# Attention's gate and queries by seven products of blocks, in a tuned one-core transformer layer

## What is computed

```python
h = rmsnorm(x, norm1_g) * (1.0 + scale1) + shift1
proj = h @ w_in
q_r, k_r, v_r, g_r, q_d, k_d, v_d, gates = split_projection(proj)
gate_r, gate_d = jnp.split(jax.nn.sigmoid(gates + b_gate), 2, axis=-1)
...                                        # rotary positions on q and k of the latent tokens
branch_r = (jax.nn.silu(g_r) * y_r) @ w_ret_out      # y_r: retention, normalised by head
branch_d = o_d @ w_diff_out                          # o_d: differential attention of q_d, k_d, v_d
mix = (gate_r * branch_r + gate_d * branch_d) @ w_o
x = x + gate1 * mix
ffn = (silu(h2 @ w_ffn_gate) * (h2 @ w_ffn_up)) @ w_ffn_down
x = x + gate2 * ffn
```

## Time and profile before

| | |
|---|---|
| median of 3 runs | 1299.69 us (1299.42 to 1299.79) |
| the profiled execution, its own time | 1299.46 us |
| its span | 1297.8 us |
| PE busy | 1259.1 us, 97% |
| DVE busy | 798.2 us, 62% |
| ACT busy | 486.7 us, 38% |
| POOL busy | 300.7 us, 23% |
| PE clock granted | full speed in all 40 slices |
| chain that ended last | 90% on PE |

### The profile page before, as it was taken

The page is one execution under the profiler, slowest core; times in us unless marked ns, Lnnn a source line. Parts: engine busy times, 40 slices in busy tenths (PEclk is TensorE's granted clock), DMA queues, the critical chain, the costliest instruction groups (busy, mean ns, idle before and its releaser), DMA issues.

```text
span 1297.8 us, 19779 instructions
## 1 busy us (share of the span) xinstructions
PE 1259.1 (97%) x7734; PEld 1152.0 (89%) x7734; DVE 798.2 (62%) x1297; ACT 486.7 (38%) x813; POOL 300.7 (23%) x264
## 2 busy tenths in 40 slices
PE   4999999999999999999999999989999999999997
PEld 2698888899999999988788899889998999889986
DVE  4654121477657743374798844478973789557966
ACT  5452233344321122223777622245441344313434
POOL 1002000311000111110799400004510445005500
PEclk9999999999999999999999999999999999999999
DMA  9634222154434434451200234311333133222222
GB/s 309 210 98 138 65 65 82 41 157 136 129 132 130 146 98 130 114 178 50 82 2 1 82 98 146 93 38 33 98 98 97 33 97 99 97 65 66 90 89 81
DMA packets 87394, 129.59 MB, mean 100 GB/s; under 512 B 3529, under 2 KB 64450, under 8 KB 87186
## 3 DMA queue, kind: packets, MB, share of 16 engines
q1 hardware_dynamic: 77024, 95.69, 23.1%
q0 software_dynamic: 8960, 31.68, 8.1%
q10 hardware_dynamic: 1330, 1.10, 0.3%
HBM read 117.43 MB, written 4.73 MB: 94 GB/s over the span
## 4 chain that ended last, share of the span: by engine, by line
PE 90%; DVE 4%; ACT 3%; POOL 1%; issue 1%; DMA 1%; ACTq 0%; DVEq 0%
PE psum L431 31%; PE psum L468 28%; PE psum L687 18%; PE psum L1240 2%; PE psum L1224 1%; PE psum L417 1%; PE psum L1199 1%; PE psum L617 1%; PE psum L1049 1%; POOL probs L989 1%; DVE w_lo L400 1%; DMA rows<-in_diff_subln_g 1%; PE psum L1157 1%; PE psum L1197 1%; POOL probs L995 1%
## 5 line engine op out<-in xcount | busy, mean ns | idle before, releaser
L400 DVE TENSOR_TENSOR w_lo<-w_raw,w_hi 128x2048 fp32r<-128x2048 f32 x57 | 130.6, 2291 | 191.6 <-ACT w_hi L395 189.2
L395 ACT ACTIVATE w_hi<-w_raw 128x2048 fp32r<-128x2048 f32 x57 | 108.8, 1909 | 173.9 <-PE psum L468 107.8
L431 PE MATMUL psum<-h_hi,w_lo 128*128 128x320 f32 x672 | 154.7, 311 | 0.0
L431 PE MATMUL psum<-h_lo,w_hi 128*128 128x320 f32 x672 | 153.1, 309 | 0.0
L431 PE MATMUL psum<-h_hi,w_hi 128*128 128x320 f32 x672 | 153.1, 309 | 0.0
L468 PE MATMUL psum<-w_hi,hid 128*128 128x512 f32 x440 | 135.6, 389 | 0.0
L431 PEld LDWEIGHTS psum<-h_hi,w_hi 128*128 128x128 f32 x672 | 112.4, 188 | 0.0
L431 PEld LDWEIGHTS psum<-h_hi,w_lo 128*128 128x128 f32 x672 | 111.8, 188 | 0.5 <-issue 0.4
L431 PEld LDWEIGHTS psum<-h_lo,w_hi 128*128 128x128 f32 x672 | 112.2, 188 | 0.0
L687 PE MATMUL psum<-h_hi,seven_lo 128*128 128x320 f32 x320 | 98.9, 309 | 1.1 <-DVE silu_g L2296 1.1
L687 PE MATMUL psum<-h_lo,seven_hi 128*128 128x320 f32 x320 | 98.9, 309 | 0.0
(11 more groups left out here) (311 smaller groups left out, 2754.7 us busy)
## 6 DMA issues: line engine op xcount, KB each, us to landing
w_raw<-in_w_in SPq DMA_DIRECT2D x32, 1024.0 KB, 5.6
ada_b<-in_w_ada POOLq DMA_DIRECT2D x32, 512.0 KB, 4.4
w_raw<-in_w_ffn_gate SPq DMA_DIRECT2D x11, 1024.0 KB, 5.3
w_raw<-in_w_ffn_up SPq DMA_DIRECT2D x11, 1024.0 KB, 5.3
ada_a<-in_w_ada SPq DMA_DIRECT2D x8, 1024.0 KB, 13.6
w_raw<-in_w_ffn_down SPq DMA_DIRECT2D x8, 1024.0 KB, 5.1
w_raw<-in_w_ret_out SPq DMA_DIRECT2D x4, 1024.0 KB, 5.2
swapped<-qk_d POOLq DMA_DIRECT2D x32, 128.0 KB, 2.5
```

The source lines that it names most:

```text
L395: act.activation(w_hi[s][:, :, :], w_raw[s][:, :, :], ACT.Copy).then_inc(w_hi_done, 1)
L400: dve.tensor_tensor(w_lo[s][:, :, :], w_raw[s][:, :, :], w_hi[s][:, :, :].bitcast(F32), ALU.subtract).then_inc(w_lo_done, 1)
L431: last = pe.matmul(bank(4 * par + 2 * j + h, HALF), w[:, k, cs], x[:, k, h * HALF:(h + 1) * HALF], start=(k == 0 and n == 0), stop=(k == K ...
```

## The change

`gate_d` and `q_d` are made of seven products, as the up phases are. `ret_out` is moved ahead of `gate_d`. Retention's normalised output is transposed after the second unit of `gate_r` instead of after the fourth. `k_d` takes a set of modulation's vectors in place of `gate_d`. POOL forms the sums of token blocks of `h` in ten subtractions or additions of 128x1280, two of them between each pair of `load_ada` of `ret_out`, and it also multiplies the queries by the cosine. `gate_d`, `qk_d`, `od_hi`, `od_lo`, `v_d`, the rotary tables and the rows of the gates get new addresses, and the gate rows are loaded in two DMAs.

```diff
-          ("gate_r", 4, "act", "act"), ("gate_d", 4, "act", "act"), ("ret_out", 4, "dve", "dve"),
-          ("q_d", 4, "act", "act"), ("k_d", 4, "act", "act"), ("v_d", 4, "act", "act"),
+          ("gate_r", 4, "act", "act"), ("ret_out", 4, "dve", "dve"), ("gate_d", 4, "dve", "dve"),
+          ("q_d", 4, "dve", "dve"), ("k_d", 4, "act", "act"), ("v_d", 4, "act", "act"),
...
-ADA_FIRST = {"gate_r": 0, "gate_d": 4, "ret_out": 8, "v_d": 12}
+ADA_FIRST = {"gate_r": 0, "ret_out": 4, "k_d": 8, "v_d": 12}
+SEVENS = ("gate_d", "q_d", "up0", "up1", "up2")
+GATED = ("gate_d", "q_d")
...
-            pe_dense(pe, "gate_r", pe_T_unit, h_hi, h_lo, first=1)
             pe.wait_ge(y_gated, RH)
-            pe_T_and_dense(pe, "yg", y_nat, "gate_d", h_hi, h_lo)
+            pe_T_and_dense(pe, "yg", y_nat, "gate_r", h_hi, h_lo, i=1)
             pe_dense(pe, "ret_out", pe_T_unit, yg_hi, yg_lo)
-            pe_dense(pe, "q_d", pe_T_unit, h_hi, h_lo)
+            for unit in gated_units:
+                pe_seven(pe, *unit)
             pe_dense(pe, "k_d", pe_T_unit, h_hi, h_lo)
...
+            def add_token_terms(first, end):
+
+                for n in range(first, end):
+                    out, x, y, op = terms[n]
+                    pool.wait_ge(h_sum_step, n) if n else pool.wait_ge(n2t["yg"]["ps"], KT)
+                    pool.tensor_tensor(out, x, y, op).then_inc(h_sum_step, 1)
...
+            add_token_terms(0, 2)
+            for i in range(2):
+                for par in range(2):
+                    load_ada("ret_out", i, par)
+                    add_token_terms(2 + 4 * i + 2 * par, 4 + 4 * i + 2 * par)
+
+            def turn_queries(i, par):
+
+                swap_halves("q_d", qk_d, P // 4, 4, 0, i, par, swapped_d)
+                x = qk_d[:, 4 * i + 2 * par:4 * i + 2 * par + 2, 0:LAT]
+                pool.tensor_tensor(rope_tmp_d[:, :, :], x, rope_d[:, 0:1, :].to_broadcast([P, 2, LAT]), ALU.mult).then_inc(rope_mul, 1)
+
+            for n, unit in enumerate(gated_units):
+                if n == 1:
+                    pool.wait_ge(ada_step, 16 * 9)
+                    pool.dma_start(rope_d[:, :, :], a["const_rope_diff"].rearrange("a p t -> p a t")).then_inc(ld_rope, 16)
+                weight_sums(*unit)
+                if n >= 6:
+                    turn_queries(*gated_units[n - 2][1:])
+                last_weight_sum(*unit)
+            turn_queries(1, 0)
+            pool.wait_ge(mm_done, ready("q_d", 1, 1, 1))
+            load_ada("k_d", 0, 0)
+            turn_queries(1, 1)
...
+            act_split(act, unit_of("ret_out", 1, 0) + 1, 1)
+            for place in range(1, 4):
+                high_of_h_sum(place)
+            prefill("gate_d", (B11, B21, T1, B22), ready("ret_out", 1, 0, 1))
+            prefill("gate_d", (T2, T4, T3), ready("ret_out", 1, 1, 1))
...
+            def gated_unit(n):
...
+                def after_third():
+                    if following:
+                        weights_low(following, (T1, B22, T2))
+                    if n >= 5:
+                        rotate_q(*gated_units[n - 1][1:])
+                    if not following:
+                        dve_split(dve, unit_of("k_d", 0, 0), 0)
...
+            dve.wait_ge(ld_rope, 32)
+            for n in range(len(gated_units)):
+                gated_unit(n)
+            dve_split(dve, unit_of("k_d", 0, 0) + 1, 1)
+            ada_partial("k_d", 0, 0)
+            rotate_q(1, 1)
```

More of the change, by code:

```diff
@@ L142, in ready, with seven_index, is_first_of_sums @@
     return i * 4 + (2 * FIRST[name] + 2 * par + j + 1 + AHEAD)
-def seven_index(third, i, par):
-    return sum(COUNT[f"up{n}"] for n in range(third)) + 2 * i + par
+def seven_index(name, i, par):
+    return sum(COUNT[other] for other in SEVENS[:SEVENS.index(name)]) + 2 * i + par
+def is_first_of_sums(name, i, par):
+    return (i, par) == (0, 0) and name in ("gate_d", "up0")
 def first_tile(third, i):
@@ L1288, in _ @@
                     pe_norm2_and_dense(pe)
-                for unit in units_of(third):
+                for unit in units_of(f"up{third}"):
                     pe_seven(pe, *unit)
@@ L1563, in _ @@
             set_table(ACT.Sigmoid)
             act.wait_ge(norm["normy"]["scaled"], 1)
-            dense_after_split("gate_r", gate("gate_r", mixT, 0))
-            act_to_T(act, "yg", yg_hi, gn_gain)
-            dense("gate_d", gate("gate_d", gate_d, KT))
-            dense("ret_out", lambda i, par: None)
-            dense("q_d", copy_T("q_d", qk_d, 0, DHD ** -0.5))
+            for h in range(RH):
+                normalize_head(h)
+            gate_of_retention(0, 0)
+            act_split(act, unit_of("gate_r", 0, 1) + 1, 0)
@@ L2024, in gated_ret @@
                     dve.tensor_tensor(x, T_tile(4 * par + 2 * j), x, ALU.mult).then_inc(freed["dve"], 1)
-            dense("ret_out", gated_ret)
-            ada_partial("v_d", 0, 0)
-            dve.wait_ge(ld_rope, 32)
-            dense("q_d", rotate("q_d", qk_d, 4, 0, 4, 128))
-            dense("k_d", rotate("k_d", qk_d, 8, DH, 4, 128 + 256))
+            first = gated_units[0]
+            dve_split(dve, unit_of("ret_out", 0, 0) + 1, 1)
+            ada_partial("ret_out", 0, 0)
+            gated_ret(0, 0)
@@ L2031, in _ @@
+            for i in range(2):
+                for par in range(2):
+                    rotate_k(i, par, during_rotation(i, par))
             dense_wide("v_d", nothing)
@@ L2332, in _ @@
                     pending = (0, 0)
-                units = units_of(third)
+                units = units_of(f"up{third}")
                 for n, unit in enumerate(units):
```

448 lines of the change are left out of this document (293 added, 155 removed).

## The result

The changed kernel takes 1305.84 us (median of 5, 1305.39 to 1306.51), the kernel before 1299.69. The ratio is 1.0047, 95% interval 1.0033 to 1.0061: 0.5% slower, where 1291.7 was forecast and 1287.5 to 1297.5 was the range. The profiled execution took 1305.45 us, its span is 1303.8.

What follows compares the result with a forecast made beforehand. The prediction took PE, busy 97% of the span, as the bound. From 1299.46 us, -14.1 + 1.5 + 0.7 + 0 + 3.3 + 0.8 = -7.8 gave 1291.7 us, range 1287.5 to 1297.5.

Steps and rivals of the forecast that it cites:

- Products: Eight units of `gate_d` and `q_d` at seven products, 12.32 us each instead of 14.09: 14.1 us less.
- Retention's output two units earlier: End of `gate_r`'s second unit: ACT and DVE finish the heads with 11 us of room, so 0.
- Last unit of `ret_out`: POOL's token sums delay DVE's low parts and modulation's sums, so PE waits 1.5 us; bounds 0 and 14.
- rival (c): `ret_out`: token sums take 4.7 us, PE waits in every unit, 13.7 us in all; 1303.9 us, chance 0.07.
- First unit of `gate_d`: The rotary table lands late for DVE's read at PE's sixth product: 0.7 us, bounds 0 and 1.5.
- Units of `gate_d` and `q_d`: POOL and DVE are nearly full beside PE, but parts are made a unit ahead: 0, bounds 0 and 5.
- From `q_d` to `k_d`: Rotation on DVE stands before the split of the key weights, so PE waits 3.3 us; bounds 2.5 and 6.
- First key unit: Modulation's sums end late behind DVE's reads and split and POOL's cosine product: 0.8 us, bounds 0 and 2.6.
- (b): Query units overflow on POOL and DVE, three units 1.7 us late each, 5 us more: 1296.7 us, chance 0.15.
- rival (a): POOL hides: modulation's sums don't wait for it, leaving 2.8 us at the split and 0.3 in `gate_d`; 1288.5, chance 0.18.

Runs made afterwards that it cites:

- sums_first: mended with two low parts of the second `gate_d` unit moved behind the first unit's reads on DVE; 1287.46 us, ratio 0.9903.
- ret_end: Changed kernel with DVE's order at the end of `ret_out` changed: modulation's sums ahead of the first two low parts; 1304.61 us, ratio 1.0038.
- late_load: Changed kernel with the 1 MB load of the second key unit's weights held until the swaps have landed; 1300.72 us, ratio 1.0007.
- rot_last: Changed kernel with DVE's query rotations behind each unit's last two reads and low parts, the last behind the key weights' split; 1294.28 us, ratio 0.9954.
- undo_rot: mended with rot_last undone, so rotations stand ahead of the last reads and the split again; 1305.48 us, ratio 1.0041.
- mended: all_edits with DVE's wait for the rotary table moved from ahead of the first `gate_d` unit to the first rotation; 1289.52 us, ratio 0.9926.
- rot_load: rot_last with the 1 MB load of the third key unit's weights held until modulation's columns have landed; 1294.84 us, ratio 0.9958.
- split_first: Changed kernel with only the split of the first key unit's weights moved ahead of the rotation on DVE; 1305.56 us, ratio 1.0046.
- rot_ret: rot_last with ret_end's order at the end of `ret_out`; 1293.65 us, ratio 0.9955.
- rot_ret_load: rot_last with ret_end's order and rot_load's held load; 1292.37 us, ratio 0.9946.
- copy_early: rot_ret_load with ACT's first copy ahead of the high parts and DVE's first read ahead of two low parts in `gate_d`; 1293.97 us, ratio 0.9956.
- cos11: rot_ret_load with the last query pair's cosine product on DVE, behind modulation's sums, instead of on POOL; 1289.57 us, ratio 0.9920.
- all_edits: rot_ret_load with the edits of copy_early and cos11 as well; 1291.03 us, ratio 0.9932.
- no_hold: all_edits without the held load of the third key unit's weights; 1290.47 us, ratio 0.9929.

## Why the prediction was wrong, step by step

- **Products, -14.1: right.** Units of the changed kernel that wait for nothing start 12.32 us apart (403.46, 415.78, 428.10). Without waits of note (sums_first) the kernel is 12.1 us faster: 14.1 less 0.7 of waits, with 1.3 left that no row names.
- **Retention's output two units earlier, 0: right.** PE shows one wait of 0.2 there.
- **Last unit of `ret_out`, 1.5: 1.9 measured, plus 1.5 of clock.** Of the two token sums in a unit the first took 3.0 to 3.2 us (3.1 assumed), the second, in the second and third unit, 4.9 beside DVE's split. That is rival (c)'s rate for one of two, and modulation's sums waited for POOL besides (rows below). In the third unit the sums ended at 370.83, 0.2 us before PE asked. That no wait came there was luck as much as reckoning. In the last unit the two token sums ran alone (3.11 each), and the wait was the forecast's. The half clock behind it was not in the sum.
- **First unit of `gate_d`, 0.7: 0.3.** The table was issued at 394.45 and took 3.9 us, not 5.2; it came before DVE had done the low parts ahead of the read (398.7). PE came late too, by its half clock. In ret_end, at full clock, PE waited 0.6 for this read, behind the same low parts and not for the table. So the size was about right and the cause was another.
- **Units of `gate_d` and `q_d`, 0: 2.6.** The chain named was the right one (rotation, last two reads, ACT's copy, T2), and its time was wrong: the reads ended 8.3 us into the last unit, not 4. DVE's 12.0 us had a rotation at 2.5, and the first took 4.5; it had low parts at 0.89 in the mean, and the one beside POOL's product took 4.11.
- **From `q_d` to `k_d`, 3.3 with bounds 2.5 and 6: this is the step that failed. 10.1, and 2.4 of clock.** It had the order right, the split behind the rotation. It set the rotation's start at 10.5 us into the unit, and it was 19.8 (478.5 to 498.3). 4.2 of these 9.3 us are the late issue: 10.2 into the unit instead of 6, because the previous rotation, late by POOL's holding and by its own swap, held the reads that free ACT. No run takes these two apart. 5.1 are the landing, 9.6 after the first issue instead of 4.5. That 4.5 came from the earlier trace rows, a swap with no weight load beside it (the load issued at 456.1 had landed when it began). late_load gives 5.3 for the same swap with the load held, so the row was nearly right for its neighbourhood and was carried into another. What the runs show in its place: a rotation whose swap is used 9.6 us after its issue holds the reads and the split behind it, and the order alone is worth 11.6 us (rot_last) to 16.0 (undo_rot against mended). The upper bound of 6 should have been worked out with the 1 MB load that T3's low part releases at just this point.
- **First key unit, 0.8: 0,** since PE came so late itself. In rot_last, where PE is on time, it is 1.5, within the bounds.

The second unit of `ret_out` in the changed kernel, POOL and DVE:

```profile
344.79 4.91 POOL L1053 TENSOR_TENSOR h_sum<-h_hi,h_sum 128x1280 f32<-128x1280 f32 x1
...
346.79 3.31 DVE L1904 TENSOR_SCALAR ada_acc<-ada_b,silu_c 128x256 f32<-128x256 f32 x2
```

The sum of the additions was 6.3, and 20.3 were given back. Of the rivals none had the right place: (b) gave the query units 5 us and got 2.6; the slower case was to come from token sums. What was missing was a slower case for the rotation itself: in-order waiting on a DMA that shares the engines with a load. One support of rival (a) was misread: the read of 0.49 in the earlier trace rows ran while POOL was idle (POOL had nothing for 2.23 us before 1056.32). The claim itself holds, by a row of the changed kernel: the read at 398.70 took 0.47 beside a weight sum of POOL from 398.19 to 399.93.

The prediction left open whether modulation's sums wait for POOL. They do: 3.31 us for 0.61 above, and 7.72 for 5.62 in ret_end. The Trainium skill (SBUF — State Buffer, "SBUF: two separate sides") has the lock for DVE operations with two SBUF inputs, or in a mode that uses both ports. The lows agree with it (4.11 us for 0.68 beside POOL's product and last weight sum), and so does the chain of fourteen. The first two of modulation's sums have one tensor of SBUF and a column of scalars and were held too (rot_load, 3.47 us for 0.61); in which mode they run no row shows.

## What to carry to other kernels

An operation that waits for a DMA goes behind everything on its in-order queue that is due earlier, reads that free another engine above all (here the place was worth 11.6 and 16.0 us); price its place by the whole queue behind it, not by its own length. Take a landing time only from a row with the same neighbours in the DMA engines, and ask which load is released at that moment. Here a wait of PE of 1.3 us or more could have a second price, the half clock behind it, and a wait that was mended by half came back one step on (split_first, ret_end): go on until the list of waits is empty, or read little into the medians between.

## What the runs showed of the hardware

Of the clock: behind waits of 1.3 to 2.4 us PE ran at 0.50 for about 3 us in some executions and not in others, with the same code at that place. rot_last and rot_ret differ only at the end of `ret_out`. Both wait 1.5 us for the first key unit's sums of modulation, at 507 and 506 us, and this is the clock behind it, in rot_last and then in rot_ret:

```profile
508.00:511.00 3.00, 3.00 (x22) 3.00 (x22) 2.68 (x4) 2.63 (x3) 1.04 (x3) 1.00 0.59 182
508.00:511.00 3.00, 3.00 (x13) 3.00 (x12) 2.33 (x3) 2.07 (x2) 2.15 (x4) 0.50 0.71 210
```

So it is with mended and undo_rot behind their wait of 2.4 us at 401 (1.00 and 0.75 from 401 to 404). Behind the wait of 1.9 us at the end of `ret_out` the clock fell in all six traces that have it, behind the 1.7 us of ret_end's order in none of four. The scatter of the runs points the same way, but weakly: the five kernels with two waits of 1.3 us or more and a time near 1293 (rot_last, rot_ret, rot_load, rot_ret_load, copy_early) spread over 3.0 to 4.1 us at mean clocks of 0.994 to 0.999; those with one or none (cos11, all_edits, no_hold, mended, sums_first) over 0.7 to 2.3, at 0.996 to 0.999. What decides it in one execution stays open.

Of the DMA engines: four swaps of 128 KB land in 2.5 to 2.7 us, and in 7.0 with 1 MB on the other queue beside them.

Of DVE and POOL: in these traces either can hold the other. A low part of 0.68 us took 4.11, modulation's chain 7.72 instead of 5.62, and a token sum of POOL 4.9 instead of 3.0, while DVE's reads of PSUM kept their 0.47 to 0.49.
